# Which operand is held in the array: the second expert table's sum turned round, in a two-layer trunk on one core

## The reference, cut to what matters

```python
def block(xt):                                  # xt: tokens x D
    ...
    g = jax.nn.softmax(top, axis=-1)            # tokens x heads x 16 chosen experts
    ue = u_tab[eidx]
    a = jax.nn.gelu(jnp.einsum('thkd,td->thk', ue, xt))
    ve = v_tab[eidx]
    return jnp.einsum('thk,thkd->td', g * a, ve)
...
x = x + g2[:, None, :] * _peer(h2, w_pq[l], sub_keys[l], u_tab[l], v_tab[l])
```

## Time and profile before

| | |
|---|---|
| time, median of 3 runs | 4209.31 us (4208.45 to 4211.87) |
| time of the profiled execution | 4210.23 us |
| its span | 4208.7 us |
| TensorE busy | 4106.4 us, 98% of the span |
| VectorE busy | 2558.4 us, 61% |
| ScalarE busy | 1349.5 us, 32% |
| granted TensorE clock, mean | 0.990 |
| sum over the second table | 1407 to 2110 us and the same again in the second layer, about 703 us each |

### The profile page before, as it was taken

One profiled execution on the slowest core, in us unless ns is written; L12 is line 12 of the kernel. 1 busy time (PEld: TensorE's weight loads), 2 busy tenths in 40 slices (PEclk: granted clock), 3 DMA queues, 4 the chain that ended last, 5 costly groups with the idle time before them and its releaser, 6 DMA issues.

```text
span 4208.7 us, 59564 instructions
## 1 busy us (share of the span) xinstructions
PE 4106.4 (98%) x19236; PEld 3360.7 (80%) x19236; DVE 2558.4 (61%) x4515; ACT 1349.5 (32%) x1569; POOL 452.8 (11%) x778
## 2 busy tenths in 40 slices
PE   6999899999999999999999999999999999999998
PEld 4777688888888888888867777888888888888886
DVE  6456587856665455555564466887566645555555
ACT  3333333344444211111133333333444442111111
POOL 0001000001111111111100010000111111111110
PEclk9999999999999999999999999999999999999999
DMA  6443233345555655555434433333455565555553
GB/s 242 141 149 139 91 127 127 126 144 175 181 190 167 246 196 203 202 207 204 169 138 158 134 135 103 125 130 130 151 171 190 180 204 215 205 195 208 202 207 117
DMA packets 187686, 707.50 MB, mean 168 GB/s; under 512 B 24176, under 2 KB 24224, under 8 KB 178496
## 3 DMA queue, kind: packets, MB, share of 16 engines
q1 hardware_dynamic: 105984, 383.83, 25.8%
q0 software_dynamic: 81600, 322.43, 22.9%
HBM read 557.26 MB, written 148.90 MB: 168 GB/s over the span
## 4 chain that ended last, share of the span: by engine, by line
PE 94%; DVE 3%; issue 1%; DMA 1%; ACT 1%; DVEq 0%; ACTq 0%; POOL 0%; SPq 0%; POOLq 0%
PE ps L395 16%; PE ps L397 16%; PE ps L396 16%; PE ps L865 11%; PE ps L866 11%; PE ps L864 11%; PE ps L847 5%; PE ps L696 1%; PE ps L772 1%; PE ps L416 1%; PE ps L752 1%; DMA mod<-in_w_mod 1%; PE ps L816 1%; PE ps L791 1%; PE ps L792 1%
## 5 line engine op out<-in xcount | busy, mean ns | idle before, releaser
L395 PE MATMUL ps<-mov,whl 128*128 128x512 f32 x2880 | 1159.1, 402 | 59.2 <-DVE whl L383 29.8
L397 PE MATMUL ps<-mov,whl 128*128 128x512 f32 x2880 | 1126.3, 391 | 0.0
L396 PE MATMUL ps<-mov,whl 128*128 128x512 f32 x2880 | 1126.0, 391 | 0.0
L383 DVE TENSOR_TENSOR whl<-raw,whl 128x1024 fp32r<-128x1024 f32 x648 | 792.5, 1225 | 546.3 <-ACT whl L373 527.6
L373 ACT CAST whl<-raw 128x1024 fp32r<-128x1024 f32 x648 | 683.6, 1056 | 1129.6 <-PE ps L866 1100.7
L865 PE MATMUL ps<-wgthl,whl 128*128 128x512 f32 x2048 | 804.9, 393 | 0.0
L864 PE MATMUL ps<-wgthl,whl 128*128 128x512 f32 x2048 | 798.9, 390 | 2.1 <-issue 2.1
L866 PE MATMUL ps<-wgthl,whl 128*128 128x512 f32 x2048 | 800.8, 391 | 0.0
L395 PEld LDWEIGHTS ps<-mov,whl 128*128 128x128 f32 x2880 | 543.1, 189 | 193.3 <-issue 47.2
L397 PEld LDWEIGHTS ps<-mov,whl 128*128 128x128 f32 x2880 | 543.0, 189 | 117.7
L396 PEld LDWEIGHTS ps<-mov,whl 128*128 128x128 f32 x2880 | 544.4, 189 | 106.0 <-issue 2.4
(11 more groups left out here) (214 smaller groups left out, 3167.0 us busy)
## 6 DMA issues: line engine op xcount, KB each, us to landing
raw<-in_uT_tab SPq DMA_DIRECT2D x256, 512.0 KB, 3.3
raw<-in_v_tab SPq DMA_DIRECT2D x256, 512.0 KB, 3.6
expert_spill<-hst POOLq DMA_DIRECT2D x256, 256.0 KB, 2.3
weight_spill<-stage POOLq DMA_DIRECT2D x32, 2048.0 KB, 11.9
gt<-weight_spill POOLq DMA_DIRECT2D x64, 1024.0 KB, 6.3
hin<-expert_spill POOLq DMA_DIRECT2D x256, 256.0 KB, 3.0
raw<-in_w_in SPq DMA_DIRECT2D x72, 512.0 KB, 4.7
raw<-in_w_mod SPq DMA_DIRECT2D x64, 512.0 KB, 3.6
```

Of the source, the lines that this page charges most:

```text
L383: nc.vector.tensor_tensor(whl[:, m % RING, 1], raw[:, raw_n(m) % RAW], whl[:, m % RING, 0].bitcast(F32), ALU.subtract).then_inc(lo_done, 1)
L395: nc.tensor.matmul(ps[:, m % 2], w[:, 0, k], src[:, 0, k], start=(k == 0), stop=False)
L396: nc.tensor.matmul(ps[:, m % 2], w[:, 0, k], src[:, 1, k], start=False, stop=False)
L397: mm = nc.tensor.matmul(ps[:, m % 2], w[:, 1, k], src[:, 0, k], start=False, stop=(k == KC - 1))
```

## The change

The operands of the sum over the second table change places. The stationary operand becomes 128 tokens of `wgthl`, the moving one 512 columns (four feature chunks, adjacent in the slot) of the table panel in `whl`. The result has tokens on the partitions: bank `2 * t + half` holds token tile `t` (of 4) by the half `half` (of 2) of the features. There are still 24 matmuls per panel (2 halves x 4 token tiles x 3 products), of the same shapes, with the same semaphores before the panel and after it.

Since `x_sb` has features on the partitions, the sum is turned round at the end of each layer. ScalarE copies the banks of token tiles 0 and 2, VectorE those of 1 and 3, from PSUM to a new tile `otok` (128 x 4 x 1024), which lies where `gt` was. TensorE turns it in 32 transposes of 128 x 128 back into the banks, and VectorE's addition to `x_sb` waits for these (`otok_turned`) instead of for the chunks of the last panel. `v_done` now counts the finished banks, seven per layer as before.

```diff
+    otok = sb("otok", [P, TT, D], at=pick_at)
...
+    otok_act, otok_dve, otok_turned = sem("otok_act"), sem("otok_dve"), sem("otok_turned")
...
                     w = whl[:, (M_V + j) % RING]
-                    for c in range(KC):
-                        nc.tensor.matmul(ps[:, c], w[:, 0, c], wgthl[:, j % 2, 0], start=first and j == 0, stop=False)
-                        nc.tensor.matmul(ps[:, c], w[:, 0, c], wgthl[:, j % 2, 1], start=False, stop=False)
-                        mm = nc.tensor.matmul(ps[:, c], w[:, 1, c], wgthl[:, j % 2, 0],
-                                              start=False, stop=last and j == 3)
-                        if last and j == 3 and c < KC - 1:
-                            mm.then_inc(v_done, 1)
+                    for half in range(2):
+                        hi, lo = (w[:, b, 4 * half:4 * half + 4].rearrange("p k c -> p (k c)") for b in range(2))
+                        for t in range(TT):
+                            o = ps[:, 2 * t + half]
+                            ghi, glo = (wgthl[:, j % 2, b, t * P:(t + 1) * P] for b in range(2))
+                            nc.tensor.matmul(o, ghi, hi, start=first and j == 0, stop=False)
+                            nc.tensor.matmul(o, ghi, lo, start=False, stop=False)
+                            mm = nc.tensor.matmul(o, glo, hi, start=False, stop=last and j == 3)
+                            if last and j == 3 and (half, t) != (1, TT - 1):
+                                mm.then_inc(v_done, 1)
                     mm.then_inc(gemm_done, 1)
...
             sum_panels(P - 4, last=True)
+            for c in range(KC):
+                if c % 4 == 0:
+                    pe.wait_ge(otok_act, l * 4 + c // 2 + 2)
+                    pe.wait_ge(otok_dve, l * 4 + c // 2 + 2)
+                bank = c % 4 * 2 + c // 4
+                for t in range(TT):
+                    mm = nc.tensor.transpose(ps[:, bank, t * P:(t + 1) * P], otok[:, t, c * P:(c + 1) * P], ident[:])
+                mm.then_inc(otok_turned, 1)
...
+            act.wait_ge(w_ready, l * P + P)
+            for half in range(2):
+                for t in (0, 2):
+                    if (half, t) == (1, TT - 1):
+                        act.wait_ge(gemm_done, 1 + l * M_ALL + M_ALL)
+                    else:
+                        act.wait_ge(v_done, l * (2 * TT - 1) + half * TT + t + 1)
+                    nc.scalar.copy(otok[:, t, half * S:(half + 1) * S], ps[:, 2 * t + half]).then_inc(otok_act, 1)
...
             sum_panels(P // 8 - 1, last=True)
+            for half in range(2):
+                for t in (1, 3):
+                    if (half, t) == (1, TT - 1):
+                        dve.wait_ge(gemm_done, 1 + l * M_ALL + M_ALL)
+                    else:
+                        dve.wait_ge(v_done, l * (2 * TT - 1) + half * TT + t + 1)
+                    nc.vector.tensor_copy(otok[:, t, half * S:(half + 1) * S], ps[:, 2 * t + half]).then_inc(otok_dve, 1)
             for c in range(KC):
-
-                if c < KC - 1:
-                    dve.wait_ge(v_done, l * (KC - 1) + c + 1)
-                else:
-                    dve.wait_ge(gemm_done, 1 + l * M_ALL + M_ALL)
-                nc.vector.scalar_tensor_tensor(x_sb[:, c], ps[:, c], mod[:, 5 * KC + c:5 * KC + c + 1], x_sb[:, c],
+                dve.wait_ge(otok_turned, l * KC + c + 1)
+                bank = c % 4 * 2 + c // 4
+                nc.vector.scalar_tensor_tensor(x_sb[:, c], ps[:, bank], mod[:, 5 * KC + c:5 * KC + c + 1], x_sb[:, c],
                                                ALU.mult, ALU.add).then_inc(x_added, 1)
```

## The result

The changed kernel takes 4244.06 us, the median of 4 runs (4239.68 to 4248.77), beside 4210.25 us for the kernel before, the median of 4 runs taken along with it; the ratio is 1.0081, with a 95% interval of 1.0063 to 1.0098. The profiled execution took 4242.29 us, its trace spans 4240.8 us. It is slower, by 34 us, outside the range that was forecast.

A forecast was written before the change was run, and what follows sets the result against it. TensorE, busy 98% of the span, was taken to bound the kernel. From 4210.2 us, 13.4 off for the sum's pace and 8.0 added at the layer ends gave 4204.8, forecast as 4204 us; range 4200 to 4225 us.

The forecast's parts named there:

- The pace: In the second table's sum, starts of the 6144 matmuls come 226.7 ns apart instead of 228.9, taking 13.4 us off.
- Rival B: Sum's matmuls stay 228.9 ns apart, through the address pair kept when exchanged or the sum's own rhythm; 4217.3 us, 27%.
- Rival C: Sum's matmuls each wait for a longer load of the held operand, 3 ns each, 18 us; 4222 or 4236 us, 15%.
- Rival D: At the layer's end the clock falls, slowing the sum of squares, 7 us in all; 4211 or 4224 us, 5%.
- The layer's end: Copies, transposes and additions after each layer's sum delay the sum of squares: 4.45 plus 3.52, 8.0 us (7.0 to 8.7).
- E: End of a layer's sum: when TensorE's next matmul could start, 0.23 us after the start of the sum's last matmul.
- the bound of 5.1: First layer's end: latest start of the sum of squares, E + 5.1 us, if TensorE's own branch holds it back.
- ScalarE's chain: First layer's end: last copy, branch, table load and first square, letting the sum of squares start at E + 4.45 us.
- The feeders: ScalarE's cast and VectorE's work per panel of the sum: 0.05 us less per panel is covered by their slack.

## Why the prediction was wrong, point by point

**The pace: wrong in direction.** The step that failed is "since the only thing that differs between rows 4 and rows 3 to 5 that the code shows is the streamed tile, and it becomes one of the good kind". All three rows hold a piece of `whl`. From them one can't tell the streamed tile's own place from its distance to the held one, and the change moves both. The runs show that the distance decides, modulo 256 bytes. From the code: `wgthl` starts 64 past a multiple of 256 counted from `whl`, so does `mrg`, and `mov` on one; every piece taken from these tiles starts a multiple of 512 further. The classes of the prediction were wrong too: it called tiles good that start on a multiple of 128, and `wgthl` put on one ran at 232.4. The exchange turned the difference from 64, the mildest of the bad values, to minus 64, among the worst. The term was -13.4 us and measured +27.3.

**Rival B** (the pace stays) named "the pair of addresses" but took it to be the same both ways round; the sign was missed. The rule of the Trainium skill that I set beside it ("TensorE: Matmul & The Clock Gate", Part 2), two independent read ports so that a load takes nothing from the running matmul, does not cover what is measured here: with the same instructions and nearly the same load time (187 to 189 ns) the pace runs from 226.7 to 233.3 ns by how the two operands lie to each other. Whether it is these two reads that meet, no run shows.

**Rival C** (slower) had the direction and a range that ends below the result; it put the price on a longer load. The loads stayed at 187 to 188 ns while the pace rose by 4.4 ns, so its mechanism was not the one at work.

**Rival D**: in the changed kernel the clock stayed at its upper level through the transposes and the wait of 1.62 us behind them. With `wgthl` moved by 448 bytes, behind a wait of 2.67 us, it fell within the sum of squares of the first layer. The prediction asked whether the transposes keep the clock up; between these two runs it is the idle time after them that differs. Whether that made the clock fall, no run takes by itself.

**The layer's end: right in mechanism, too small in size.** Copies, transposes and additions came where they were forecast (last copy E + 0.20, transposes 3.5 us, second layer E + 3.49 against 3.52). The first layer measured 5.27 us in the changed kernel, not 4.45, and lay just beyond the bound of 5.1: I took ScalarE's chain for the last one and kept TensorE's own branch for the bound, and it was that branch. The term was 8.0 us and measured 8.8.

**The feeders** had slack, as said: ScalarE and VectorE waited longer, nobody waited for them.

## What to carry to other kernels

Before an operand is exchanged or a tile moved, compute the difference of the two matmul operands' start addresses modulo 256 and read the pace of existing matmuls as start-to-start distance; a stream of 6144 matmuls turned 2 to 7 ns into 13 to 41 us here, and 192 unused bytes were worth more than the change. When two cases differ in one tile, ask whether the tile or its relation to another one differs, and look for a row that parts them. A loop's branch that used to be reached early becomes part of the path when a wait is put before it.

## What the runs showed of the hardware that was not expected

For `fp32r` matmuls of 128x128 by 128x512 back to back at full clock, the distance of starts is 226.7 ns when streamed and held operand start the same number of bytes modulo 256, 228.9 when the streamed one starts 64 further, and 232.4 to 233.3 at the other differences measured (32, 128, 192, 224). The matmul's recorded duration goes with it (389 to 395 ns), the load's doesn't. Why the best of the bad values is plus 64, and what reads collide, no run here shows. With the return to the head of the layer loop TensorE went on at E + 5.27 and E + 6.33, with straight code at E + 4.32; the first two are kernels with the same program there, and why they differ by 1.06 us is not shown. The granted clock stayed at 1.00 over an idle time of 1.62 us after the transposes and fell after one of 2.67 us.
